# Gated products of the second feed-forward with tokens on partitions, turned by VectorE in pieces of 32 partitions

## The reference, cut to what matters

```
def swiglu(h, w_gate, w_up, w_down):
    return (jax.nn.silu(h @ w_gate) * (h @ w_up)) @ w_down

h = rmsnorm(x, ln_ffn)                              # (256 tokens, 2048)
x = x + swiglu(h, w_gate, w_up, w_down)             # w_gate, w_up: 2048 x 5632, w_down: 5632 x 2048
return rmsnorm(x, final_norm)
```

## Time and profile before

| | |
|---|---|
| median of 3 runs | 2664.56 us (2661.61 to 2667.21) |
| the profiled execution: its own time, its span | 2663.23 us, 2661.4 us |
| TensorE busy (matmul; weight load) | 2615.7 us, 98%; 2346.4 us, 88% |
| GpSimd busy | 2186.5 us, 82% |
| ScalarE busy | 1263.8 us, 47% |
| VectorE busy | 1163.0 us, 44% |
| mean granted clock of TensorE | 0.996 |

### The profile page before, as it was taken

The page is one execution under the profiler, slowest core; times in us unless marked ns, Lnnn a source line. Parts: engine busy times, 40 slices in busy tenths (PEclk is TensorE's granted clock), DMA queues, the critical chain, the costliest instruction groups (busy, mean ns, idle before and its releaser), DMA issues.

```text
span 2661.4 us, 41769 instructions
## 1 busy us (share of the span) xinstructions
PE 2615.7 (98%) x16010; PEld 2346.4 (88%) x16010; DVE 1163.0 (44%) x1457; ACT 1263.8 (47%) x1530; POOL 2186.5 (82%) x889
## 2 busy tenths in 40 slices
PE   8999999999999999999999999999999999999998
PEld 8979999898888888888898888989998888888886
DVE  6767757674646464422364347712311111113223
ACT  5445465545444444444653454534544444445444
POOL 7878766777999998899899765867878888889996
PEclk9999999999999999999999999999999999999999
DMA  9998987664656665455455533634545555555553
GB/s 373 392 397 319 381 350 300 228 243 159 248 225 245 228 236 190 174 205 190 173 190 198 186 139 127 237 139 148 202 176 190 189 186 186 186 186 193 198 191 126
DMA packets 101761, 587.41 MB, mean 221 GB/s; under 512 B 11240, under 2 KB 13416, under 8 KB 45200
## 3 DMA queue, kind: packets, MB, share of 16 engines
q1 hardware_dynamic: 93600, 570.07, 57.9%
q10 hardware_dynamic: 8048, 15.74, 1.7%
HBM read 579.46 MB, written 8.40 MB: 221 GB/s over the span
## 4 chain that ended last, share of the span: by engine, by line
PE 81%; POOL 9%; issue 6%; DVE 3%; ACT 0%; DMA 0%; POOLq 0%; DVEq 0%; ACTq 0%; SPq 0%
PE ps L1315 29%; PE ps L1320 15%; POOL w_lo L551 9%; PE ps L1332 6%; PE ps L1363 4%; PE ps L1365 4%; PE ps L1274 4%; PE ps L1371 4%; PE ps L1281 4%; PE ps L1276 4%; PE ps L1337 3%; PE ps L1634 1%; PE ps L1968 1%; PE ps L1943 1%; PE ps L1434 0%
## 5 line engine op out<-in xcount | busy, mean ns | idle before, releaser
L551 POOL TENSOR_TENSOR w_lo<-raw,w_hi 128x1024 fp32r<-128x1024 f32 x884 | 2186.1, 2488 | 456.9 <-ACT w_hi L574 454.1
L574 ACT CAST w_hi<-raw 128x1024 fp32r<-128x1024 f32 x884 | 924.1, 1051 | 1108.8 <-PE ps L1320 570.3
L1315 PE MATMUL ps<-a_both,w_hi 128*128 128x512 f32 x3328 | 833.4, 392 | 0.0
L1315 PEld LDWEIGHTS ps<-a_both,w_hi 128*128 128x128 f32 x3328 | 598.6, 189 | 107.0
L1320 PEld LDWEIGHTS ps<-a_both,w_lo 128*128 128x128 f32 x3328 | 453.7, 190 | 33.1 <-POOL w_lo L551 0.8
L1320 PE MATMUL ps<-a_both,w_lo 128*128 128x256 f32 x3328 | 464.3, 282 | 0.0
L1274 PE MATMUL ps<-a_both,w_hi 128*128 128x256 f32 x1616 | 405.1, 288 | 10.9 <-issue 3.3
L1276 PE MATMUL ps<-a_both,w_hi 128*128 128x256 f32 x1616 | 398.6, 284 | 0.0
L1274 PEld LDWEIGHTS ps<-a_both,w_hi 128*128 128x128 f32 x1616 | 311.4, 193 | 14.5 <-issue 4.2
L1276 PEld LDWEIGHTS ps<-a_both,w_hi 128*128 128x128 f32 x1616 | 311.8, 193 | 0.5
L2631 DVE TENSOR_TENSOR ps<-ps,work 128x1024 f32<-128x1024 f32 x42 | 51.7, 1232 | 503.8 <-ACT work L943 503.8
(11 more groups left out here) (277 smaller groups left out, 2024.9 us busy)
## 6 DMA issues: line engine op xcount, KB each, us to landing
raw<-stream SPq DMA_DIRECT2D x440, 1024.0 KB, 4.8
arena<-ada SPq DMA_DIRECT2D x184, 512.0 KB, 6.7
work<-ada SPq DMA_DIRECT2D x8, 512.0 KB, 6.9
arena<-memT SPq DMA_DIRECT2D x4, 512.0 KB, 9.8
res<-xT SPq DMA_DIRECT2D x4, 512.0 KB, 13.4
v_spill<-arena ACTq DMA_DIRECT2D x4, 512.0 KB, 3.4
k_spill<-arena ACTq DMA_DIRECT2D x4, 512.0 KB, 7.4
rel_rows<-rel_row ACTq DMA_DIRECT2D x4, 512.0 KB
```

Source lines behind the costliest of these rows:

```text
L551: pool.tensor_tensor(w_lo[:, h % SLOTS], raw_half(h), w_hi[:, h % SLOTS].bitcast(F32), ALU.subtract).then_inc(lo_ready, 1)
L574: act.copy(w_hi[:, base % 4], raw[:, tile_slot, (base % 2) * HALF:(base % 2 + 1) * HALF]).then_inc(hi_ready, 1)
L1315: pe.matmul(acc_two(g + turned)[:, f], w_hi[:, h % SLOTS, cols(k, f)], a_both[:, c0 + k], start=first and k == 0, stop=False, skip_group_c ...
```

## The change

All 22 groups of gu use `half_N`. The sums of a group lie in two banks (`acc_tok`), tokens on partitions: for each half of the tokens 256 columns of gate and 256 of up. ScalarE takes silu straight from PSUM, one instruction of 256 columns for each half of the tokens, with the token's factor as its scale. VectorE multiplies with the up columns (`gated`) and writes the product into `work`, tokens on partitions; that frees the banks. The down stage needs features on partitions, so VectorE then turns the product with 16 transposes of 32 partitions x 128 elements (`hidden_turned`): each reads one quarter of the partitions and writes one quarter, turning four blocks of 32 x 32. `second_sums`, `both_sums` and `gate_rows` are gone from this stage, and so are the semaphore `gs_ready` and the parameter `turned`. `hidden_high` now waits for the transposes by `hid_ready`. VectorE's loop over the groups is written out; TensorE's loop covers groups 2 to 21. The wait of TensorE for the turned residual (`rt_copied`) moves from before group 2 to after group 21.

```diff
@@ -906,11 +906,7 @@
-                if name == "down":
-                    act.wait_ge(hid_ready, min(2 * n + 2, 22))
-                elif n <= 10:
-                    for G in (G0["gu"] + 2 * n, G0["gu"] + 2 * n + 1):
-                        act.wait_ge(evac[G % 2], G // 2 + 1)
+                act.wait_ge(hid_ready, (0 if name == "down" else 22) + min(2 * n + 2, 22))
                 late = 2 if name == "down" and n == 2 else 0
...
@@ -937,10 +933,9 @@
                 act.wait_ge(half_used, halves if i is None else i * 16 + halves)
-                taken = g - 1 if name == "up" else 22 + g - 3
-                if taken > 0:
-                    act.wait_ge(two_added, taken if i is None else i * 2 + taken)
-                act.copy(low_sums(g), acc_two(g + (name == "gu"))[:, :, 1, :]).then_inc(lc_ready, 1)
+                if g > 1:
+                    act.wait_ge(two_added, g - 1 if i is None else i * 2 + (g - 1))
+                act.copy(low_sums(g), acc_two(g)[:, :, 1, :]).then_inc(lc_ready, 1)
...
@@ -1174,26 +1169,34 @@
-            def gate_silu(par, g, i=None):
-                act.wait_ge(gs_ready, g + 1 if i is None else i * 2 + (g + 1))
-                act.activation(conv[:, par, 0:2, :], conv[:, par, 0:2, :], ACT.Silu).then_inc(silu_ready, 1)
+            def gate_silu(g, i=None):
+                halves = hg + 8 * g + 8
+                act.wait_ge(half_used, halves if i is None else i * 16 + halves)
+                for t in range(2):
+                    ins = act.activation(conv[:, g % 2, t, :], acc_tok(G0["gu"] + g)[:, t, 0:S], ACT.Silu,
+                                         scale=tok(0, t))
+                ins.then_inc(silu_ready, 1)
-            gate_silu(0, 0)
             his(hg + 12, 3)
             res_turned(0)
+            act.wait_ge(tok_ready, 4)
+            gate_silu(0)
             his(hg + 15, 1)
             res_turned(3)
-            gate_silu(1, 1)
-            his(hg + 19, 5)
+            his(hg + 19, 1)
+            gate_silu(1)
+            his(hg + 20, 4)
             def gate_two(g, i=None):
...
@@ -1201,12 +1204,9 @@
                     down_head("down2")
-                second_sums("gu", g, i)
+                gate_silu(g, i)
                 if g < 21:
-                    his(hg + 8 * g + 12, 2, h=h)
-                gate_silu(g % 2, g, i)
-                if g < 21:
-                    his(hg + 8 * g + 14, 2, h=h)
+                    his(hg + 8 * g + 12, 4, h=h)
...
@@ -1994,11 +1994,10 @@
-            Gg = G0["gu"]
             for n in range(7):
-                half_of("T", "gu", n, al=al_before("lnffn"))
+                half_of("N", "gu", n, al=al_before("lnffn"))
             row_sums("lnffn", (ps[:, 4, 0:S], four))
-            half_of("T", "gu", 7)
+            half_of("N", "gu", 7)
             def turn_residual(q):
...
@@ -2017,13 +2016,9 @@
                     turn_residual((11, 12, 14, 15).index(n))
-                half_of("T", "gu", n)
+                half_of("N", "gu", n)
+            groups("N", "gu", 2, 22)
             pe.wait_ge(rt_copied, 4)
-            for g in range(2, 4):
-                group_two("gu", g)
-            with pe.Fori(0, 9) as i:
-                for g in range(4, 6):
-                    group_two("gu", g, i)
             down("down2", 22)
...
@@ -2973,40 +2968,32 @@
-            def gu_sums(g):
-                return acc(G0["gu"] + g) if g < 2 else acc_two(g + 1)[:, :, 0, :]
-            def gate_rows(g, i=None):
-                if g < 2:
-                    dve.wait_ge(half_used, hg + 8 * g + 8)
-                else:
-                    both_sums(g, 22 + g - 2, i, 1)
-                dve.tensor_tensor(conv[:, g % 2, 0:2, :], gu_sums(g)[:, 0:2, :], over_chunks(row_a, 2), ALU.mult)\
-                   .then_inc(gs_ready, 1)
-            def swiglu(g, i=None):
+            def gated(g):
                 G, base = G0["gu"] + g, 25 + g + 1
-                dve.wait_ge(silu_ready, base if i is None else i * 2 + base)
-                o = hidden[:, 2 * g:2 * g + 2, :] if i is None else hidden[:, bass.ds(i * 4 + 2 * g, 2), :]
-                dve.tensor_tensor(o, gu_sums(g)[:, 2:4, :], conv[:, g % 2, 0:2, :], ALU.mult)\
-                   .then_inc(evac[G % 2], 1)
-            def gu_out(g, i=None):
-                gate_rows(g, i)
-                swiglu(g, i)
-            gu_out(0)
+                dve.wait_ge(silu_ready, base)
+                dve.tensor_tensor(conv[:, g % 2, 2:4, :], acc_tok(G)[:, :, S:2 * S], conv[:, g % 2, 0:2, :], ALU.mult)                   .then_inc(evac[G % 2], 1)
+            def hidden_turned(g):
+                G = G0["gu"] + g
+                dve.wait_ge(evac[G % 2], G // 2 + 1)
+                o = hidden[:, 2 * g:2 * g + 2, :]
+                for a in range(4):
+                    for b in range(4):
+                        x = conv[32 * a:32 * a + 32, g % 2, 2:4, :].rearrange("p t (c n) -> p c t n", c=2)
+                        y = o[32 * b:32 * b + 32].rearrange("p c (t n) -> p c t n", t=2)
+                        ins = dve.transpose(y[:, :, :, 32 * a:32 * a + 32], x[:, :, :, 32 * b:32 * b + 32])
+                ins.then_inc(hid_ready, 1)
+            def gu_out(g):
+                gated(g)
+                hidden_turned(g)
             tok_copy(0, 4)
-            for g in range(1, 4):
+            for g in range(21):
                 gu_out(g)
-            with dve.Fori(0, 8) as i:
-                for g in range(4, 6):
-                    gu_out(g, i)
-            gu_out(20)
             hidden_low(22, 0)
```

More of the change, by code:

```diff
@@ L1305, in half_chunks, with half_two @@
                 mm.then_inc(half_used, 1)
-            def half_two(h, g, c0, first, last, i=None, step=0, turned=0):
+            def half_two(h, g, c0, first, last, i=None, step=0):
                 def cols(k, f):
@@ L1314, in half_two @@
                     for f in range(4):
[L1315 removed]
+                        pe.matmul(acc_two(g)[:, f], w_hi[:, h % SLOTS, cols(k, f)], a_both[:, c0 + k],
                                   start=first and k == 0, stop=False, skip_group_check=True)
@@ L1319, in half_two @@
                     for f in range(4):
-                        mm = pe.matmul(acc_two(g + turned)[:, f, 0, :], w_lo[:, h % SLOTS, cols(k, f)],
+                        mm = pe.matmul(acc_two(g)[:, f, 0, :], w_lo[:, h % SLOTS, cols(k, f)],
                                        a_hi[:, c0 + k, :], start=False, stop=last and k == 1, skip_group_check=True)
```

15 lines of the change are left out of this document (7 added, 8 removed).

## The result

The changed kernel takes 2651.23 us, the median of five runs (2650.55 to 2651.51). The ratio to the kernel before is 0.995, with a 95% interval of 0.9938 to 0.9961: 0.5% faster. The forecast was 2650.3 us. The profiled execution took 2651.39 us with a span of 2649.2.

A forecast was written before the change was run, and what follows sets the result against it. TensorE was taken to bound the kernel, through its period per half. Savings of 2.6 us (groups 0 and 1) and 11.7 us (groups 2 to 21), summed as 14.2, gave 2664.56 - 14.2 = 2650.3 us, range 2646 to 2657.

The forecast's parts named there:

- The period: TensorE's time per half in gu groups 2 to 21: from 2.793 to 2.720 us, saving 11.7 us over 160 halves.
- the loss at each change of the stationary operand: On TensorE, the claimed reason why 24, 16 and 12 matmuls take 2.88, 2.793 and 2.720 us per half.
- Groups 0 and 1: First two groups of gu on TensorE: 16 halves going from 2.88 to 2.72 us each, 2.6 us saved.
- Cost the same: On TensorE, row sums and the turning of the residual stay in place at unchanged cost.
- the signs: What would show the forecast right in gu, including GpSimd's mean low part between 2400 and 2450 ns, 0.3 us idle each.
- the other end: Upper case for transposes slowing GpSimd in gu: 0.27 us per us, 1.4 us per group; the forecast charged 0.
- the slack: GpSimd's idle time in gu at 2.72 us per half, which VectorE may take: 2.54 us per group of 8 halves.
- The price of 0.27 us per us: GpSimd time lost per us of VectorE work with two SBUF operands, taken from down2: 15.0 us over 80 low parts.
- 5.0 to 5.8: VectorE's time in us for a group's 16 transposes in gu, without and with 0.05 us between them.
- the nearest row: Profile row used to size ScalarE's new silu of 256 columns from PSUM: 0.384 us each, 0.77 us for two.
- The tail: Passage from gu to down2: low parts of down2's first two quads start no later, and group 21's end gets lighter.
- The whole: Total saving for the kernel: 14.2 us, all on the path, 0.53% less time.

The follow-up runs named there:

- t_all: The changed kernel with all 22 groups of gu multiplied by half_T again, the rest unchanged: 2679.36 us, ratio 1.0054 to the kernel before.
- t_first: The changed kernel with only groups 0 and 1 of gu multiplied by half_T again: 2653.31 us, ratio 0.9961 to the kernel before.
- tr_four: The changed kernel with each group's 16 transposes issued four times, extra sets into unused SBUF: 2660.01 us, ratio 0.9983 to the kernel before.
- copy_six: The changed kernel with six extra VectorE copies, SBUF to SBUF, after the transposes in each of groups 2 to 19: 2650.47 us.
- sb_two: The changed kernel with two extra two-operand VectorE operations, SBUF to SBUF, after the transposes in each of groups 2 to 19: 2647.47 us.
- sb_six: The changed kernel with six extra two-operand VectorE operations, SBUF to SBUF, after the transposes in each of groups 2 to 19: 2700.38 us.
- up_n2: The changed kernel with the first block's up stage also on tokens, ScalarE issuing the rows' transfers, and group 1 ahead of ScalarE's loop: 2640.82 us.

## Why the prediction was right

- The period. The prediction took 2.72 us per half from down2: measured 2.720 in groups 2 to 21, 11.74 us against the 11.7 of the sum. t_all confirms the price of `half_T`. The reason given, "the loss at each change of the stationary operand", is rougher than the number: in `half_T` two matmuls in a row (L1274, L1276) use the same piece of weights and each still has its own load, and the 0.0034 us on each long matmul of `half_two` have no place in it.
- Groups 0 and 1: 2.32 us against 2.6, and 2.35 by t_first. The term was a little too large: 16 halves at 2.72 leave 49.15 - 43.52 = 5.63 us for the row sums and turns between them, where before 51.47 - 16 x 2.88 = 5.39 were left. "Cost the same" was wrong by 0.24 us. The restart after a turn is not the place: the first matmul behind one starts its successor 0.08 us late in before and 0.09 us late in after. Where the 0.24 us went stays open.
- GpSimd. Nothing was charged for the product and the transposes: 2396 ns against 2402 before (the signs asked for 2400 to 2450), idle 0.33 each where 0.32 was worked out. tr_four shows that this holds for four times as many. Even the other end, 1.4 us per group, would have stayed inside the slack, as copy_six and sb_two show, where GpSimd lost 1.7 and 1.6 us per group. The price of 0.27 us per us, however, was taken from recorded durations that hold waiting, and sb_six shows it to be too low.
- VectorE. 16 transposes in 5.05 us, at the lower end of 5.0 to 5.8; one takes 303 ns where 315 were estimated from sizes four and eight times as large.
- ScalarE. The silu was mis-sized: 468 ns for 256 columns where the nearest row gave 384, 0.83 us for two. L643 is another function (a square, without a scale). It cost nothing, since the next high part waits for TensorE 0.94 us longer.
- The tail: the low parts for down2's first quads took 5.93 us from 2393.64, 5.87 us before gu's end, and TensorE entered down2 without a wait. tr_four shows where this cover ends.
- The whole. 14.09 us by stretches, 14.2 predicted; 13.3 by the medians, whose interval (10.4 to 16.5 us) holds both. That gu starts at a different time in each execution is enough for the difference; the medians can't tell more.

## What to carry to other kernels

Where TensorE sets the pace and operands are stored in halves, count the matmuls, each of which has its own load of the stationary operand (15178 of both in after): the same 6144 columns took 2.88, 2.793 and 2.720 us with 24, 16 and 12 of them. If the cheaper form leaves the result turned the wrong way, let an idle engine turn it off the path: VectorE did it for nothing where TensorE's own turn would have taken 10.6 of 14.1 us. Before you fill an engine, ask which queue waits for it: the same change one block earlier lost 80 us, and gained 10 once the rows' transfers were out of the weights' queue and ScalarE's tables no longer reloaded.

## What the runs showed of the hardware

VectorE's copies and two-operand operations from SBUF to SBUF run alternately with GpSimd's low parts, one instruction each: 1.09 us with two operands and 0.55 us for a copy (1024 fp32 elements), 2.26 for the low part; transposes run beside them at no cost to either. The recorded durations hide this, since the wait of a blocked instruction lies inside its duration: the same two-operand operation (L2291) is in the trace of tr_four with 1.22 us (started at 2402.38, just ahead of a low part) and with 3.42 us (started at 2403.53, behind it). The 0.27 us per us of the prediction was such a mixture. Transposes of 32 partitions take 303 ns for 128 elements and 456 for 256 (224 of them in up_n2), and follow each other without overlap though they use different quarters of the partitions: 48 in 15.17 us, 316 ns each.
